# Two row gathers to one in the last pair of an expert-retrieval kernel, and a root of a constant ahead of the last wait

## The reference, cut to what matters

```python
def peer_ffn(x, wq, keys, u_tab, v_tab):
    ...
    def block(xt):                      # 128 tokens
        q = (xt @ wq).reshape(bn, PEER_BLOCK, PEER_HEADS, 2, PEER_DHALF)
        s = jnp.einsum('bthpd,hpnd->bthpn', q, keys).astype(jnp.float32)
        sv, si = lax.top_k(s, PEER_TOPK)
        ...
        act = jax.nn.gelu(jnp.einsum('bthkd,btd->bthk', u_tab[expert], xt).astype(jnp.float32))
        return jnp.einsum('bthk,bthkd->btd', (gate * act).astype(xt.dtype), v_tab[expert])
...
        h = h + peer_ffn(rms_norm(h, norm2_g[layer]), ...)
    return rms_norm(h, final_g)
```

## Time and profile before

| | before |
|---|---|
| median of three runs | 1678.6 us |
| span of the profiled execution (its own time, the span being all that is listed of it) | 1676.9 us |
| DMA, mean over the span | 375 GB/s |
| Pool busy | 988.9 us (59%) |
| VectorE busy | 1097.6 us (65%) |
| TensorE busy | 989.6 us (59%) |
| gathers | 512 of u, 512 of v, 512 KB each |

### The profile page before, as it was taken

How to read it: one execution, slowest core, us unless ns; L and a number is a source line. 1 busy time by engine, 2 the same in 40 slices (tenths; PEclk the granted TensorE clock), 3 DMA queues, 4 the chain that set the end, 5 groups by cost and what they waited for, 6 DMA issues and landing times.

```text
span 1676.9 us, 19109 instructions
## 1 busy us (share of the span) xinstructions
PE 989.6 (59%) x5988; PEld 589.1 (35%) x5988; DVE 1097.6 (65%) x2822; ACT 301.0 (18%) x832; POOL 988.9 (59%) x1028
## 2 busy tenths in 40 slices
PE   5887578785653335978674436888763433333334
PEld 5766467452430003655351004665440000000000
DVE  6441499977465798878647666878647767676430
ACT  4433243141100003224110003233110001000000
POOL 0000246677666667646766777556766777777764
PEclk9898779897785657989776567999886655655677
DMA  6323599999999999999999999999999999999997
GB/s 239 116 68 113 170 383 361 419 418 419 419 418 420 419 382 375 419 419 411 417 419 419 419 420 419 419 418 392 415 419 419 420 420 419 419 420 419 420 383 291
DMA packets 172613, 628.69 MB, mean 375 GB/s; under 512 B 19168, under 2 KB 19168, under 8 KB 172512
## 3 DMA queue, kind: packets, MB, share of 16 engines
q0 software_dynamic: 147456, 536.94, 79.3%
q1 hardware_dynamic: 25056, 90.53, 14.1%
HBM read 626.34 MB, written 1.05 MB: 374 GB/s over the span
## 4 chain that ended last, share of the span: by engine, by line
DMA 33%; DVE 21%; PE 16%; issue 14%; POOL 9%; DVEq 3%; ACT 2%; ACTq 0%; POOLq 0%; SPq 0%
DMA uring<-in_u_tab,small 20%; PE ps L414 16%; DMA vring<-in_v_tab,small 13%; DVE uring L1240 10%; POOL vring L1640 5%; POOL uring L1640 4%; DVE sel L1203 1%; DVE sel L1207 1%; DVE small L1211 1%; ACT gd L1325 0%; DVE sa L934 0%; DVE small L1193 0%; DVE small L1161 0%; PE ps L417 0%; DVE small L1172 0%
## 5 line engine op out<-in xcount | busy, mean ns | idle before, releaser
L1240 DVE CUSTOM_DVE_ANT_0 uring<-uring,ps 128x1024 f32<-128x1024 f32 x512 | 619.0, 1217 | 332.9 <-DMA uring<-in_u_tab,small 307.4
L1640 POOL DMA_INDIRECT uring<-in_u_tab,small x512 | 494.7, 966 | 503.3 <-DVEq L1225 198.1
L414 PE MATMUL ps<-vring,wmat 128*32 128x512 f32 x2048 | 393.3, 907 | 548.1 <-DMA vring<-in_v_tab,small 537.3
L1640 POOL DMA_INDIRECT vring<-in_v_tab,small x512 | 494.0, 965 | 167.9 <-issue 139.0
L414 PEld LDWEIGHTS ps<-vring,wmat 128*32 128x32 f32 x2048 | 78.3, 142 | 799.5 <-issue 797.0
L414 PE MATMUL ps<-hnT,wring 128*128 128x128 f32 x1536 | 191.9, 283 | 8.6 <-DMA wring<-in_w_blocks 3.4
L414 PEld LDWEIGHTS ps<-hnT,wring 128*128 128x128 f32 x1536 | 181.6, 197 | 27.5 <-issue 12.7
L414 PE MATMUL ps<-wring,hnT 128*128 128x256 f32 x448 | 111.6, 403 | 1.4 <-ACT hnT L1325 0.7
L414 PEld LDWEIGHTS ps<-wring,hnT 128*128 128x128 f32 x448 | 88.3, 204 | 26.3 <-issue 11.6
L414 PE MATMUL ps<-gd 128*128 128x128 f32 x544 | 72.2, 283 | 20.1 <-ACT gd L1325 20.1
L414 PEld LDWEIGHTS ps<-gd 128*128 128x128 f32 x544 | 67.5, 195 | 40.5 <-ACT gd L1325 24.3
(11 more groups left out here) (276 smaller groups left out, 1093.4 us busy)
## 6 DMA issues: line engine op xcount, KB each, us to landing
wring<-in_w_blocks SPq DMA_DIRECT2D x152, 512.0 KB, 7.1
uring<-in_u_tab,small POOLq DMA_INDIRECT x512, 11.6
vring<-in_v_tab,small POOLq DMA_INDIRECT x512, 11.6
wring<-in_cols SPq DMA_DIRECT2D x4, 512.0 KB, 6.4
sa<-in_rows SPq DMA_DIRECT2D x4, 512.0 KB, 6.4
h<-in_x SPq DMA_DIRECT2D x2, 512.0 KB, 5.2
keysT<-in_keys SPq DMA_DIRECT2D x2, 512.0 KB, 9.4
rows<-in_rows SPq DMA_DIRECT2D x2, 486.0 KB, 8.0
```

The lines of the kernel that those rows point to most:

```text
L414: return nc.tensor.matmul(o, a, b, start=start, stop=True, skip_group_check=True)
L1240: V.tensor_tensor_reduce(row_, row_, xp, 1.0, 0.0, ALU.mult, ALU.add, dots[:, j:j + 1]).then_inc(dot_done.sem, 1)
L1640: nc.gpsimd.indirect_dma_start(dst, None, table, bass.IndirectOffsetOnAxis(ap=index, axis=0)).then_inc(done.sem, 16)
```

## The change

It makes two edits. First, the loop body of Pool's program is cut into `u_gather(q)` and `v_gather(q)`, with the same waits and slots as before. In pairs 1 to 14 the order stays one u, one v. In pair 15 a v gather of pair 14 follows only every second u gather: 32 u and 16 v gathers. The other 16 v gathers of pair 14 and the 32 of pair 15 follow alone, 48 in a row. Second, ScalarE computes a square root of a constant into a new column, `root`, at the start of `final(1)`, ahead of its wait for the last sum. Nothing reads `root`. Its buffer `small` grows from 1376 to 1408 columns.

```diff
-    ss, rstd, eps, eps_q, eps_k = (tiny(1) for _ in range(5))
+    ss, rstd, eps, eps_q, eps_k, root = (tiny(1) for _ in range(6))
...
         def final(t):
+            if t == 1:
+                S.activation(root, eps, ACT.Sqrt)
             act.wait_ge(y_read.sem, 3 + t)
             norm_square(t, junk).then_inc(final_ss.sem, 1)
...
-        for n in range(NP + 1):
-            if n < NP:
-                pool.wait_ge(ids_ready.sem, n + 1)
+        def u_gather(q):
+            if q >= URING:
+                pool.wait_ge(dot_done.sem, q - URING + 1)
                 pool.sem_inc(pool_gate.sem, 1)
+            gather(uring[:, q % URING, :], u_tab, ids[(q // PAIR) % 2][:, q % PAIR:q % PAIR + 1], u_in[q % URING])
+
+        def v_gather(q):
+            if q >= VRING:
+                pool.wait_ge(v_used.sem, q - VRING + 1)
+                pool.sem_inc(pool_gate.sem, 1)
+            gather(vring[:, q % VRING, :], v_tab, idv[(q // PAIR) % 3][:, q % PAIR:q % PAIR + 1], v_in[q % VRING])
+
+        for n in range(NP):
+            pool.wait_ge(ids_ready.sem, n + 1)
+            pool.sem_inc(pool_gate.sem, 1)
             for j in range(PAIR):
...
+                u_gather(PAIR * n + j)
+                if n == NP - 1 and j % 2 == 1:
+                    v_gather(PAIR * (n - 1) + j // 2)
+                elif 0 < n < NP - 1:
+                    v_gather(PAIR * (n - 1) + j)
+        for q in range(PAIR * (NP - 2) + PAIR // 2, PAIR * NP):
+            v_gather(q)
```

More of the change, by code:

```diff
@@ L148, in _build @@
     wmat = sb("wmat", [P, 2, 1056])
-    small = sb("small", [P, 1376])
+    small = sb("small", [P, 1408])
     uring = sb("uring", [P, URING, D])
@@ L213, in tiny @@
         sm[0] += n
-        assert sm[0] <= 1376, sm[0]
+        assert sm[0] <= 1408, sm[0]
         return small[:, a:a + n] if dt == F32 else small[:, a:a + n].bitcast(dt)
-    ss, rstd, eps, eps_q, eps_k = (tiny(1) for _ in range(5))
+    ss, rstd, eps, eps_q, eps_k, root = (tiny(1) for _ in range(6))
     (stp, xr, th, zz, em1, kk_, s2, c2, t0, t1, t2, sin1, cosm1, are, aim, kre, kim, mag) = (tiny(8) for _ in range(18))
@@ L1641, in gather @@
                                          ).then_inc(done.sem, 16)
-        for n in range(NP + 1):
-            if n < NP:
-                pool.wait_ge(ids_ready.sem, n + 1)
+        def u_gather(q):
+            if q >= URING:
+                pool.wait_ge(dot_done.sem, q - URING + 1)
                 pool.sem_inc(pool_gate.sem, 1)
-            for j in range(PAIR):
[L1648 to L1659, removed]
+            gather(uring[:, q % URING, :], u_tab, ids[(q // PAIR) % 2][:, q % PAIR:q % PAIR + 1], u_in[q % URING])
[7 more added lines that the diff above has]
+            pool.sem_inc(pool_gate.sem, 1)
+            for j in range(PAIR):
+                u_gather(PAIR * n + j)
[5 more added lines that the diff above has]
+            v_gather(q)
 def kernel(**inputs):
```

## The result

The changed kernel takes 1712.93 us (median of four runs, 1711.15 to 1713.5); the kernel before takes 1679.8 beside it. The ratio is 1.0189, with a 95% interval of 1.0174 to 1.0204: **slower by some 32 us** (29 to 34 by the interval), where I had forecast no measurable change (1677.3 us, range 1674.5 to 1680.5). The profiled run took 1713.5 us with a span of 1711.7, against a span of 1676.9 before.

What follows compares the result with a forecast made beforehand. The prediction took the gathers, at the DMA engines' 419 GB/s, to bound the kernel: span 1676.9 - 1.3 (root) + 0 (order) = 1675.6 us, with the median 1.7 above, so 1677.3 us, range 1674.5 to 1680.5.

Steps and rivals of the forecast that it cites:

- nothing is added or removed: Pair 15's reordered gathers: still 1024 gathers, each with its old wait; only who waits when moves, net cost 0.
- the sum: Whole kernel: span 1676.9 - 1.3 + 0 = 1675.6 us, and 1.7 above it the forecast median of 1677.3 us.
- the bounds: Whole kernel: limits on the terms' costs, which put the forecast time between 1676.5 and 1678.3 us.
- all four rivals: Whole kernel: idle bytes are time 1672.8 (0.08); refilling spared 1676.5 (0.14); u ring binds 1684.2 (0.08); root saves nothing 1678.6 (0.05).
- The rate as the bound: Whole kernel: gathers bound it, DMA engines mostly moving 418 to 420 GB/s; only idle DMA time or the end can be gained.
- The root: Program end, ScalarE: the table load moves ahead of the wait, out of line with the store, saving 1.3 us.
- The changeover: Switch to v gathers alone, 16 v gathers earlier: Pool waits 4.8 us, landings continue every 1.25 us, net 0.
- T: Time of the changeover to v gathers alone in the new order, put near 1593 us.
- The rival that took the 4.5 us of idle DMA bytes for time: Changeover: mean DMA rate sets the end, so all 4.5 us come back, 1672.8 us; chance 0.08.
- The u ring: Early pair 15: Pool waits on dots about 1 us, landings shorten from 11.3 to about 10.4 us, cost 0.
- One sign of mine: Pair 15: the rate stays at 419 GB/s while u gathers' landings fall from 11.3 to about 10.4 us.
- The rival that the ring binds: Pair 15: landings stay near 12.5 us, so u slots return late, 6.9 us in all, 1684.2 us; chance 0.08.

Runs made afterwards that it cites:

- the fourth set: Runs on one unhindered chip, kernel before 1680.58 us: u ring alone moved 128 bytes 1680.29, change at 1440 columns 1678.93, Pool's order alone 1679.87 us.

## Why the prediction was wrong, point by point

**The step that failed.** I wrote of the reordered gathers that "nothing is added or removed", and went through waits, queues and orders. The diff's first hunk, the larger `small`, I did not price at all. I treated memory that nothing reads as free. It moved three rings by 128 bytes, and that cost 32.6 us by the run that did nothing else (1713.13 against 1680.51). In the terms of the sum, the start from the 1676.9 us of the kernel before took for granted that all outside the two edits stays as it was, and the larger buffer had no term. The working of the sum, the bounds and all four rivals take the DMA engines' rate of 419 GB/s as given; none could reach 1713. What I took for the kernel's fixed limit depended on where its buffers lay.

**The rate as the bound.** That the gathers bound the kernel was right, and it is the reason for the size of the loss: 2.4% less rate gave 1.9% more time. What I did not see is that Pool's own pace lies right beside it. From 1371 to 1612 us of the kernel before, which is pairs 13 to 15, Pool is never idle for over 0.31 us ahead of a gather. It issues one every 1.24 us, or 423 GB/s, with now and then a longer one. The transfers keep up with little change in the queue (10 to 12.6 us from issue to landing). So a faster DMA engine would have gained next to nothing in this stretch, and a slower one costs at once. A slip in the reading of the earlier trace rows: the DMA engines are busy nine tenths from the sixth slice on, not the seventh, and in the last slice it is seven.

**The root: right in the trace.** 1.22 us from squares to root where it was 2.50, so 1.28 us for the forecast 1.3, and no load. The time does not show it by itself: with both edits at the old size the ratio is 0.9997, and at 1440 columns 0.9989. In the fourth set the kernel with order and root takes 0.9 us less than the one with the order alone (1678.93 against 1679.87), which is within the spread of the runs. The run of the root alone fell on a hindered chip.

**The changeover: right in kind, near in size.** I had T at 1593, a wait of 4.8 us up to 1606.5, and nothing won or lost. With the order alone Pool's next gather behind the wait starts at 1607.52 after 4.26 us, and the time is that of the kernel before within 0.1%. The landings did pass through the gap: in the second run of both edits at the old size a gather from ahead of the wait lands at 1610.02 and the fourth behind it, issued after the wait, at 1615.02, so 1.25 us each. From the first dot of pair 15 to the last v group it is 121.1 us with the order alone, against 121.5 before. The rival that took the 4.5 us of idle DMA bytes for time (0.9973) is outside the interval of 0.9987 to 1.0008.

**The u ring: right in kind, one size off.** Pool did wait on dots early in pair 15 (1.25 us with the usual 0.30, so 0.95), and landings did shorten from 11.3, but not to the 10.4 us that I had: to 8.3 us, and later 9.4. The difference is the second wait, of 2.48 us, which the trace puts down to no engine. It stands before the same gather in the changed kernel (2.53 us before 1586.05); I have no cause for it. One sign of mine failed: the rate in pair 15 did not stay at 419 but was 414 GB/s from 1533 to 1604 us. Over 71 us that is an estimate of 0.8 us in bytes, taken out of the queue, and no time shows it. The rival that the ring binds (1.0041) is refuted as well.

## What to carry to other kernels

Read every line of a diff for what it moves, and a change in the size of a buffer above all: it shifts all that is allocated behind it. Where a kernel lives at the DMA engines' full rate, try the place of the rings that rows are written to, with unused columns ahead of them, and compare the steady rate of before and after ahead of any theory about order; here that one row pointed away from the order, and the run with nothing but the larger buffer settled it. And when a chip is held back by something else, the best slices still show a ceiling that the times hide.

## What was not expected of the hardware

In these runs the place to which the rows are written sets the rate of 4096-byte gathers into SBUF: with all rings moved by 0 or 256 bytes it is 419 GB/s, by 64 or 128 bytes 409. No other moves were run, so a period of 256 bytes fits but is not proven. In the trace 99.0% of the 4096-byte packets of Pool's queue last 159 ns in the kernel before, and their mean is 161.1 ns. With `small` at 1408 and nothing else it is 40.7%, and the mean is 164.8. With only the v and weights' rings moved, it is 95.8%.

The Trainium skill (DMA: Bandwidth & Descriptors, How a descriptor splits into AXI transactions) says that a transfer is cut into pieces of up to 256 bytes, each of which must start at a multiple of 256, and that bytes fetched ahead of the start cost beats of 32 bytes although they are not used. Worked out from this for 4096 bytes that start elsewhere, these are estimates: 17 pieces instead of 16, or 6% more. In beats it is 132 instead of 128 (3.1%) for a start 128 bytes behind such a multiple, and 130 (1.6%) for one 64 bytes behind. The page tells this of reads, and here the side that is written had moved. The runs agree with it in kind, in that 256 bytes cost nothing. That 64 bytes cost as much as 128 is like the count of pieces and unlike that of beats; the size, 2.4%, is that of neither. Which absolute addresses the rings have is not to be seen in the trace. The sizes in the source ahead of `uring` add up to 120880 bytes, 48 more than a multiple of 256, and what the allocator rounds or reserves is not known. So that good places are multiples of 256 is a guess.

The second surprise is that a full rate of 419 to 420 GB/s survives when badly placed rows alternate with well placed ones. That fits an engine whose slower side has some slack against the other, but no run looked at the two sides apart, so that is argued and not shown.
